# Two-block model on one core: where the root of the first norm is applied

## The reference

```python
def rms_norm(x, gain):
    xf = x.astype(jnp.float32)
    xf = xf * lax.rsqrt(jnp.mean(xf * xf, axis=-1, keepdims=True) + RMS_EPS)
    return (xf * gain.astype(jnp.float32)).astype(x.dtype)
...
        hn = rms_norm(h, norm_mix_g[layer])
        proj = hn @ w_in[layer]
        p_dil = proj[..., :3 * WIDTH_DIL]...   # 8 heads, dilated attention
        p_na = proj[..., 3 * WIDTH_DIL:]...    # 8 heads, neighbourhood attention
```

## Time and profile before

| | us |
|---|---|
| median of three runs | 2589.7 (2587.46 to 2589.85) |
| the profiled execution | 2588.41 |
| its span in the trace | 2586.6 |
| TensorE busy in that span | 2424.3 (94%) |
| DVE, POOL, ACT busy | 1030.0, 700.8, 575.8 |

### The profile page before, as it was taken

How to read it: one execution, slowest core, us unless ns; L and a number is a source line. 1 busy time by engine, 2 the same in 40 slices (tenths; PEclk the granted TensorE clock), 3 DMA queues, 4 the chain that set the end, 5 groups by cost and what they waited for, 6 DMA issues and landing times.

```text
span 2586.6 us, 27460 instructions
## 1 busy us (share of the span) xinstructions
PE 2424.3 (94%) x10966; PEld 1748.0 (68%) x10966; DVE 1030.0 (40%) x1771; ACT 575.8 (22%) x780; POOL 700.8 (27%) x456
## 2 busy tenths in 40 slices
PE   5999999998998599999799999999899999999997
PEld 4888799997875244444444338644588888888885
DVE  6894044445423011111667866611422122122124
ACT  3001255566622111110121004100211011011011
POOL 2333433444430200000304860001133332332321
PEclk9999999999999799999899999779899999999998
DMA  3232122222414677821501110001111111111111
GB/s 137 69 118 94 34 77 69 67 86 78 142 62 163 234 274 270 318 91 74 191 33 49 73 57 25 9 17 41 41 49 37 61 49 37 61 46 39 54 32 75
DMA packets 74349, 228.67 MB, mean 88 GB/s; under 512 B 5169, under 2 KB 36913, under 8 KB 69233
## 3 DMA queue, kind: packets, MB, share of 16 engines
q1 hardware_dynamic: 55712, 141.19, 15.7%
q0 software_dynamic: 12896, 61.09, 6.6%
q10 hardware_dynamic: 5616, 24.64, 2.3%
HBM read 173.42 MB, written 53.48 MB: 88 GB/s over the span
## 4 chain that ended last, share of the span: by engine, by line
PE 91%; DVE 4%; issue 2%; DMA 1%; ACT 1%; POOL 0%; SPq 0%; DVEq 0%; POOLq 0%; ACTq 0%
PE ps L679 13%; PE ps L681 13%; PE ps L683 13%; PE ps L639 11%; PE ps L844 8%; PE ps L770 7%; PE ps L747 4%; PE ps L860 4%; PE ps L756 3%; PE ps L691 2%; PE ps L661 2%; PE ps L935 1%; PE ps L954 1%; PE ps L835 1%; PE ps L1032 1%
## 5 line engine op out<-in xcount | busy, mean ns | idle before, releaser
L679 PE MATMUL ps<-work_part 128*128 128x512 f32 x1472 | 454.0, 390 | 7.2 <-POOL work_part L520 7.2
L683 PE MATMUL ps<-work_part 128*128 128x512 f32 x1472 | 453.2, 389 | 0.0
L518 POOL CAST work_part<-ring 128x1024 fp32r<-128x1024 f32 (+2 forms) x108 | 105.6, 978 | 1039.2 <-PE ps L683 639.0
L681 PE MATMUL ps<-work_part 128*128 128x512 f32 x1120 | 344.8, 389 | 0.0
L679 PEld LDWEIGHTS ps<-work_part 128*128 128x128 f32 x1472 | 275.6, 188 | 65.1 <-issue 8.4
L683 PEld LDWEIGHTS ps<-work_part 128*128 128x128 f32 x1472 | 276.3, 188 | 57.5
L639 PE MATMUL ps<-work,ring 128*128 128x512 f32 x640 | 278.7, 596 | 1.4 <-DVE work L2018 1.4
L520 POOL TENSOR_TENSOR work_part<-ring,work_part 128x1024 fp32r<-128x1024 f32 (+2 forms) x108 | 241.9, 2240 | 8.6
L681 PEld LDWEIGHTS ps<-work_part 128*128 128x128 f32 x1120 | 210.3, 188 | 43.6
L639 PEld LDWEIGHTS ps<-work,ring 128*128 128x128 f32 x640 | 122.2, 191 | 155.1 <-issue 153.2
L844 PE MATMUL ps<-work 128*128 x496 | 219.1, 595 | 0.6 <-issue 0.3
(11 more groups left out here) (323 smaller groups left out, 2984.3 us busy)
## 6 DMA issues: line engine op xcount, KB each, us to landing
work<-w_moe SPq DMA_DIRECT2D x16, 3072.0 KB, 11.7
ring<-w_up_units SPq DMA_DIRECT2D x44, 512.0 KB, 3.3
ring<-w_in_units SPq DMA_DIRECT2D x42, 512.0 KB, 3.3
x_slots<-hT SPq DMA_DIRECT2D x31, 512.0 KB, 3.5
work<-x_slots POOLq DMA_DIRECT2D x31, 512.0 KB, 4.5
y_slots<-work ACTq DMA_DIRECT2D x31, 512.0 KB, 2.6
ring<-w_down_units SPq DMA_DIRECT2D x24, 384.0 KB, 3.0
s_turns<-work ACTq DMA_DIRECT2D x8, 1024.0 KB, 3.9
```

Source lines behind the costliest of these rows:

```text
L518: pool.tensor_copy(WHI[n % 2][:, 0:cols], w).then_inc(whi_ready, 1)
L679: pe.matmul(ps[:, c], whi[:, w], hi[k][:, c], start=(k == 0), stop=False)
L681: pe.matmul(ps[:, c], whi[:, w], lo[k][:, c], start=False, stop=False)
L683: mm = pe.matmul(ps[:, c], wlo[:, w], hi[k][:, c], start=False, stop=(k == len(hi) - 1))
```

## The change

The inputs are no longer multiplied by the inverse root. They are split with the gain alone: ACT computes the high part as input times gain right after each square, and DVE the low part as input times gain minus high part. The sum of squares, root and inverse are still computed, but later: `norm_sum` runs on TensorE behind `first_pair`, DVE inverts behind its chain of tiny operations, and `norm_root` runs behind projection tile 6. ACT copies the spread root from PSUM to SBUF (`RB`, laid over 1024 of the constants' columns that only the second block needs). DVE multiplies the eight value tiles (in place of ACT's copy to `Wp[24]`) and the sixteen query and key tiles by it, behind the S5 tables. Columns 739 to 1890 of the constants are not loaded at the start but by POOL before head 2. The other constants come first, in two transfers, then weight unit 0, two input tiles, unit 1, the other six input tiles.

```diff
+        RB = cst[:, MCOLS["low"]:MCOLS["low"] + S]
...
-        n_mix = add_norm(Hp, "norm_mix", (Wp[19:22] * 3)[0:8], Wp[22:25], 8, take(2),
-                         parts=(BHI, [hTr[t][:, :] for t in range(NT)]))
-        U_QKV = [take(1) for m in range(16)]
+        U_QKV = [take(1) for m in range(2)]
+        mix_use = take(1)
+        U_QKV += [take(1) for m in range(2, 7)]
+        n_mix = add_late_norm(Hp, "norm_mix", [Wp[22], Wp[23], Wp[15]], mix_use, take(1), (BHI, [hTr[t][:, :] for t in range(NT)]))
+        U_QKV += [take(1) for m in range(7, 16)]
...   (SP)
-            for i in range(4):
+            def load_x(i):
                 sp.dma_start(hT[:, 2 * i:2 * i + 2, :], xT[:, 2 * i:2 * i + 2, :]).then_inc(x_loaded[i], 16)
-                if i == 0:
-                    sp.dma_start(cst[:], params).then_inc(cst_loaded, 16)
+            for a, b in ((0, MCOLS["low"]), (MCOLS["gkup"], NCOL)):
+                sp.dma_start(cst[:, a:b], params[:, a:b]).then_inc(cst_loaded, 16)
             for u, src in enumerate(units):
+                if u == 1:
+                    load_x(0)
+                if u == 2:
+                    for i in range(1, 4):
+                        load_x(i)
...   (POOL, per head h)
+                if h % 2 == 0:
+                    pool.wait_ge(qk_scaled, h + 2)
                 if h == 0:
-                    pool.wait_ge(qkv_ready, 16)
                     pool.wait_ge(mm_done, done(U_VT[6]))
+                if h == 2:
+                    pool.wait_ge(qk_scaled, 16)
+                    pool.wait_ge(vT_ready, 8)
+                    a, b = MCOLS["low"], MCOLS["gkup"]
+                    pool.dma_start(cst[:, a:b], params[:, a:b]).then_inc(cst_again, 16)
...   (TensorE)
-            norm(n_mix)
             first_pair(U_IN, U_QKV[0], U_QKV[1], BHI, xlo_ready, n_mix["lo0"], n_mix["parts"][1])
+            norm_sum(n_mix)
             for m in range(2, 16):
                 parts_tile(U_IN + m, U_QKV[m], *n_mix["parts"])
+                if m == 6:
+                    norm_root(n_mix)
...   (ACT)
-            norm(n_mix, x_gate)
-            norm_parts(n_mix)
+            for t in range(NT):
+                x_gate(t)
+                if t >= 3:
+                    act.wait_ge(sq_added, n_mix["add0"] + t - 2)
+                act.activation(n_mix["scratch"][0 if t == 0 else 1 + (t - 1) % 2], Hp[t], ACT.Square).then_inc(sq_ready, 1)
+                act.activation(BHI[t], Hp[t], ACT.Copy, scale=par("norm_mix", t)).then_inc(xhi_ready, 1)
...   (ACT, copies of the projections)
-                    act.activation(Wp[24], PS[bank(U_VT[m - 16])][:, :], ACT.Copy).then_inc(vT_ready, 1)
+                if m == 6:
+                    act.wait_ge(root_spread, n_mix["spread"] + 1)
+                    act.activation(RB, PS[bank(n_mix["root_use"])][:, :], ACT.Copy).then_inc(roots_copied, 1)
...   (DVE)
-            norm(n_mix)
+            def part_lo(c, t):
+                dve.wait_ge(sq_ready, c["sq0"] + t + 1)
+                dve.wait_ge(xhi_ready, c["lo0"] + t + 1)
+                dve.scalar_tensor_tensor(out=c["parts"][1][t], in0=c["src"][t], scalar=par(c["gain"], t),
+                                         in1=c["parts"][0][t].bitcast(f32), op0=ALU.mult, op1=ALU.subtract).then_inc(xlo_ready, 1)
+            for t in range(NT):
+                if t >= 1:
+                    norm_add(n_mix, t)
+                part_lo(n_mix, t)
...   (DVE, between the chain of tiny operations and the S5 tables)
+            norm_inverse(n_mix)
...   (DVE, behind the S5 tables)
+            dve.wait_ge(roots_copied, 1)
+            for m in range(8):
+                if m >= 1:
+                    dve.wait_ge(mm_done, done(U_V[m - 1]))
+                dve.wait_ge(mm_done, done(U_VT[m]))
+                dve.tensor_tensor(Wp[24], PS[bank(U_VT[m])][:, :], RB, ALU.mult).then_inc(vT_ready, 1)
+                for i in (m, 8 + m):
+                    dve.wait_ge(qkv_ready, i + 1)
+                    dve.tensor_tensor(Wp[i], Wp[i], RB, ALU.mult).then_inc(qk_scaled, 1)
```

More of the change, by code:

```diff
@@ L152, in build @@
         qkv_ready, vT_ready = sem("qkv_ready"), sem("vT_ready")
-        inverse_ready, root_spread = sem("inverse_ready"), sem("root_spread")
+        inverse_ready, root_spread, roots_copied = sem("inverse_ready"), sem("root_spread"), sem("roots_copied")
+        qk_scaled, cst_again = sem("qk_scaled"), sem("cst_again")
         scores_ready, exp_done, pT_ready, heads_done, f_ready = (
@@ L214, in build, with add_late_norm @@
         xn_base = [0]
+        def add_late_norm(src, gain, scratch, use, root_use, parts):
+            norms.append(dict(src=src, gain=gain, scratch=scratch, tiles=8, use=use, sq0=sq_base[0], add0=add_base[0],
+                              index=len(norms), spread=sum(c["root_use"] is not None for c in norms), parts=parts,
+                              lo0=split_base[0], late=sum("late" in c for c in norms), root_use=root_use))
+            c = norms[-1]
+            split_base[0] += 8
+            sq_base[0] += 8
+            add_base[0] += 7
+            emptied[use] = (std_ready, len(norms))
+            emptied[root_use] = (roots_copied, c["late"] + 1)
+            return c
         def add_norm(src, gain, dst, scratch, tiles, use, root_use=None, parts=None, spread=True):
@@ L718, in norm @@
                 norm_root(c)
-            pe.wait_ge(cst_loaded, 16)
-            norm(n_mix)
+            pe.wait_ge(cst_loaded, 32)
             first_pair(U_IN, U_QKV[0], U_QKV[1], BHI, xlo_ready, n_mix["lo0"], n_mix["parts"][1])
+            norm_sum(n_mix)
             for m in range(2, 16):
                 parts_tile(U_IN + m, U_QKV[m], *n_mix["parts"])
+                if m == 6:
+                    norm_root(n_mix)
             for m in range(9):
@@ L913, in _ @@
                 pe.wait_ge(conv_ready, c + 1)
+                if c == 0:
+                    pe.wait_ge(cst_again, 16)
                 for gate in range(2):
@@ L1102, in x_gate @@
                     act.wait_ge(x_loaded[t // 2], 16)
-            norm(n_mix, x_gate)
-            norm_parts(n_mix)
-            act.wait_ge(normed, 1)
+            act.wait_ge(cst_loaded, 32)
+            for t in range(NT):
[4 more added lines that the diff above has]
+                act.activation(BHI[t], Hp[t], ACT.Copy, scale=par("norm_mix", t)).then_inc(xhi_ready, 1)
+            act.activation(root_of_eps[:, n_mix["index"]:n_mix["index"] + 1], epsc[:], ACT.Sqrt)
+            norm_std(n_mix)
             for m in range(24):
@@ L1111, in _ @@
                             act.wait_ge(turns_stored[i], 32)
-                    if m > 16:
-                        act.wait_ge(mm_done, done(U_V[m - 17]))
-                    act.wait_ge(mm_done, done(U_VT[m - 16]))
-                    act.activation(Wp[24], PS[bank(U_VT[m - 16])][:, :], ACT.Copy).then_inc(vT_ready, 1)
                 n = U_QKV[m] if m < 16 else U_V[m - 16]
@@ L1434, in norm @@
                 norm_apply(c, then)
-            dve.wait_ge(cst_loaded, 16)
-            norm(n_mix)
-            dve.wait_ge(cst_loaded, 16)
+            def part_lo(c, t):
[3 more added lines that the diff above has]
+                                         in1=c["parts"][0][t].bitcast(f32), op0=ALU.mult, op1=ALU.subtract).then_inc(xlo_ready, 1)
+            dve.wait_ge(cst_loaded, 32)
+            for t in range(NT):
+                if t >= 1:
+                    norm_add(n_mix, t)
+                part_lo(n_mix, t)
             free = list(range(40))
```

## The result

| | before | after |
|---|---|---|
| median of five runs, us | 2589.7 (2587.46 to 2591.23) | 2567.38 (2556.32 to 2569.35) |
| ratio | | 0.9902, 95% interval 0.9877 to 0.9927 |
| the profiled execution | 2588.41 | 2567.38 |
| its span | 2586.6 | 2565.3 |

The kernel is faster by 22.3 us where 20.2 were forecast (2569.5 against 2589.7). The interval of the ratio reaches from 18.9 to 31.9 us less. By the ratio the time is 0.9902 x 2589.7 = 2564.3, and that lies 1.2 us under the lower end of my range; the median of 2567.38 lies inside it. The two differ because the ratio here is that of the means, 2563.96 and 2589.30: of the five runs of the changed kernel two took 2556.32 and 2558.62, and no run of the kernel before was that far under its median. The chain of waits has kept its shape: TensorE holds 91% of it, as in the earlier trace rows.

A forecast was written before the change was run, and what follows sets the result against it. TensorE was taken to bound the kernel; start -21.6, sums 0, spread +1.9 and junction +0.3 gave -19.4 us, hence 2569.5 us. The range was 2565.5 to 2576 us, the main case's own 2567 to 2573.

The forecast's parts named there:

- What bounds the kernel: Whole kernel: TensorE, busy 94% of the span; a change pays only where it stands idle or loses matmuls.
- The start: First projection matmul at 14.2 instead of 35.81, a gain of 21.6 us (20.7 to 22.6).
- the landing of the loads: Kernel start: at 0.425 MB per us, the first input pair lands at 8.35 and weight unit 1 at 9.6.
- The rule of the Trainium skill: At the start and value tiles: POOL contends with DVE instructions having two SBUF inputs, so the first low part waits.
- `first_pair`: First projection stretch: stays 24.3 us, with twelve slow matmuls kept; other counts would change the sum by -0.6 to +1.0.
- What returns to TensorE: Work put back into TensorE's chain behind the start: norm_sum at cost 0 and norm_root at about 1.9 us.
- The sums: The 16 norm_sum matmuls fit the 2.40 us gap behind `first_pair`: cost 0, at worst 1.3 us.
- The spread: The four norm_root matmuls behind projection tile 6 cost about 1.9 us, cold 3.8.
- The DVE chain: Tiny operations, inversion and diagonal end at 85.8; TensorE reaches norm_root at 95.5, leaving 9.7 us spare.
- The junction: From the last value tile to the first bias addition: +0.3 us, between -0.7 and +2.0.
- The sum: Whole kernel: -21.6 + 0 + 1.9 + 0.3 = -19.4 us, giving 2569.5 us.
- The gain is taken back later: Rival, chance 0.07: the granted clock falls elsewhere in later work, half of the gain goes, 2580 us.

The follow-up runs named there:

- delay_b: The changed kernel with 18 settings of an unused buffer on POOL holding back the first load: 2586.5 us, 1.0001 of the kernel before.
- quick_start: The changed kernel with only gains, then weight units, ahead of the input, ACT's table loaded early, query and key products behind value tiles 0 to 3: 2565.97 us.
- root_after_4: The changed kernel with norm_root behind projection tile 4 instead of 6, banks moved accordingly: 2584.51 us, 0.9991 of the kernel before.
- early_qk: The changed kernel with the sixteen query and key products done behind value tiles 0 to 3, four each: 2566.64 us, 0.9919 of the kernel before.
- delay_s: The changed kernel with three settings of an unused buffer on POOL holding back the first load: 2570.69 us, 0.9935 of the kernel before.
- before_new_loads: The kernel before with the new order of loads alone: 2588.66 us, 1.0004 of the kernel before.

## Why the prediction had the path right, and what it missed

**What bounds the kernel: right.** 20.3 us of idle start became a first score 18.6 earlier, and the 1.7 between are accounted for below; delay_b gives the gain back.

**The start (-21.6 forecast, -20.3 measured).** The mechanism held: input, then ACT, then a low part that POOL holds up, then TensorE. The term that was off is the landing of the loads: unit 1, whose split sets the start in my sum, at 9.6 forecast and 10.85 measured, and the input pair at 8.35 and 9.62. I took 0.425 MB per us from the first byte on; the first weight unit, 1.13 MB into the stream, was ready for POOL at 7.11, where that rule gives 5.9, so all of the miss was there before the input began. Whether the two narrow transfers of constants ahead cause it is open: in quick_start only 40 columns of constants go ahead, and the pair lands at 9.44 where the same rule gives 8.2. The rule of the Trainium skill ("GPSIMD Engine Reference", "Key points") on the shared interface agreed with the traces: the low part took 2.25, and the products cost POOL 0.9 each.

**`first_pair`.** 23.4 us instead of 24.3: eight slow matmuls until 19.0, not twelve. That is -0.85, a little past the better end of my bounds (-0.6). It holds for this trace alone: the other three of the changed kernel took 24.1 to 24.7.

**What returns to TensorE.** The sums cost nothing, as said. The spread cost 1.75 (four matmuls, and a slower first pair behind them) where 1.9 was the term. The DVE chain was done at 86.5 against 85.8 forecast, TensorE came at 97.6 against 95.5; root_after_4 shows that this slack is real and what it would cost to lose it.

**The junction (+0.3 forecast).** The last turned tile came 0.7 earlier by DVE than by ACT, as worked out, the strip 0.6 too late: the first score gained 0.7, and the bias addition, 2.22 behind it instead of 1.38, lost 0.84: +0.1.

**The sum.** -20.3 - 0.85 + 1.75 + 0.1, and 1.6 for the slow stretch at 43 to 47, is -17.7; the bias addition moved from 314.33 to 296.58, 17.75. The other three traces start 0.3 to 0.9 later and have a longer `first_pair` but no such stretch; their marks are the same within 0.5. (In the prediction the better end of the bounds adds up to -22.1, not -22.2.) So the change itself is worth 18 to 19 us, a little less than the 19.4 of my sum.

**The step that failed: the rival "The gain is taken back later", and with it the lower end of the range.** It let the granted clock behind the start take half of the gain away (0.07) and never let it add any, so the lower end had nothing in it for the clock. Its grounds were "the stretches shown all have the clock at 1.00" and "the three runs agree within 2.4 us". The stretches shown end at 226 us; the page before has a mean of 0.965 and this row of the clock, in tenths, for 40 equal slices of the span (9 is 90% or more):

```profile
PEclk9999999999999799999899999779899999999998
```

And three runs were too few. Over all comparisons 73 runs of the kernel before have a median of 2587.8 and reach from 2574.6 to 2593.6, 14 of them under 2580; 23 runs of the changed kernel have a median of 2566.5 and reach from 2556.3 to 2571.9, four of them under 2560. The times go with the mean granted clock (0.968 to 0.971 in the low ones, 0.962 to 0.967 in the others). So in both kernels about one run in five is some ten microseconds faster. That the first comparison drew two of five on one side and none of five on the other, and so came out at 0.9902, was chance; the later ones gave 0.9914, 0.9926 and 0.9934, all inside the range. The range should have reached to 2560. That the mean of the four ratios (0.9919) lies so close to the forecast (0.9922) is likewise more than these runs can vouch for: the marks say 18.1 to 19.0 us, the forecast 20.2.

**What stays open.** The medians are 19.3 to 22.4 under the kernel before, and the marks 18.1 to 19.0. The difference of up to 4 us lies behind the mark and is within the intervals. In the traces it comes from stretches at 1.2 GHz that are longer or shorter, in different places each time; whether a mark at 294 makes the longer ones rarer is not settled. None of the profiled executions is one of the low ones, so where those ten microseconds lie isn't shown either.

## What to carry to other kernels

When the engine that bounds the kernel starts late, list both chains that must meet at its first instruction, and order the loads for the later one: moving the root away was worth 7 us here, the same with the loads in the right order 20. Factors that commute with a matmul can be applied behind it, on an engine with slack, but look where the new operations meet a second engine on the same memory. And take the scatter of the kernel from many runs before setting the near end of a range, not from three.

## What was unexpected of the hardware

- An idle stretch of TensorE can cost more than itself: 11.35 us of waiting gave a first score 13.3 us later, with the clock at 0.85 over the 20 us behind.
- A short gap can do it too, but not each time. Behind the 2.5 us with 16 one-column matmuls the clock was 0.60 from 43 to 47 in one trace of the changed kernel; its three other traces have no such stretch there, those of early_qk and delay_s have one, and so has before_new_loads behind a gap of the same length without work. These are the four traces in which `first_pair` was shortest (23.4 to 23.5 us against 23.8 to 24.7 in the others), so the sums alone don't bring it about.
- POOL and DVE hold each other up for about an instruction: POOL's two splits took 6.9 us alone and 11.3 beside DVE operations with two inputs in SBUF, and a low part that began inside a subtraction ended 1.08 us behind it, close to its own 1.27. Beside the bias addition from PSUM at 314.33 POOL's subtraction lost nothing (2.40).
- One kernel's runs lie in two groups ten microseconds apart, with the mean granted clock (0.968 to 0.971 against 0.962 to 0.967) the only other thing that differs in their records.
